# Weight buffers at four offsets modulo 128 bytes, and 13 warm-up products in place of 6

## What is computed

```python
def reference(x, mem, ..., c_2, ..., w_down_2):
    x = first_block(x, mem, g_mix, w_in, ...)     # retention + forgetting attention, w_out,
                                                  # cross attention to 256 memory rows, gated FFN (2816)
    return second_block(x, c_2, w_ada_2, ...)     # modulation from c, grouped attention + window pooling,
                                                  # w_out, FFN with a 3-tap convolution (2 x 2816)
```

## Time and profile before

| | us |
|---|---|
| median of three runs | 1438.58 |
| the three runs | 1436.09, 1438.58, 1439.15 |
| the profiled execution, first to last instruction | 1441.5 |
| TensorE busy in it | 1390.7 |
| VectorE busy | 818.5 |
| ScalarE busy | 616.9 |
| GpSimd busy | 604.1 |

### The profile page before, as it was taken

How to read it: one execution, slowest core, us unless ns; L and a number is a source line. 1 busy time by engine, 2 the same in 40 slices (tenths; PEclk the granted TensorE clock), 3 DMA queues, 4 the chain that set the end, 5 groups by cost and what they waited for, 6 DMA issues and landing times.

```text
span 1441.5 us, 17910 instructions
## 1 busy us (share of the span) xinstructions
PE 1390.7 (96%) x6628; PEld 1110.5 (77%) x6628; DVE 818.5 (57%) x1235; ACT 616.9 (43%) x857; POOL 604.1 (42%) x448
## 2 busy tenths in 40 slices
PE   8999999999999999999999889988999999999999
PEld 6877955788876888888888667864678888888887
DVE  5334948365342487777789994579355554553000
ACT  5455228543353343343431113578435555453111
POOL 3344320474521444544453444331344455556453
PEclk9999999999989999999999998999999999999999
DMA  7222221142210243333445553210121322222322
GB/s 262 86 87 95 80 67 51 59 149 106 88 68 1 90 170 149 131 140 140 156 162 188 205 190 107 83 59 30 59 88 59 116 87 87 100 104 88 117 88 88
DMA packets 28769, 154.20 MB, mean 107 GB/s; under 512 B 2992, under 2 KB 4144, under 8 KB 14512
## 3 DMA queue, kind: packets, MB, share of 16 engines
q1 hardware_dynamic: 28720, 153.52, 29.8%
HBM read 151.41 MB, written 2.10 MB: 106 GB/s over the span
## 4 chain that ended last, share of the span: by engine, by line
issue 41%; PE 30%; POOL 24%; DVE 4%; DMA 1%; POOLq 0%; ACT 0%; SPq 0%
POOL wlo L362 24%; PE lin L1326 10%; PE lin L1328 9%; PE lin L1327 9%; DVE small L992 1%; DVE expd L1003 1%; DMA raw<-w_slabs 1%; PE lin L1529 0%; PE att L1382 0%; DVE xl L872 0%; DVE win L1216 0%; DVE small L996 0%; POOLq L371 0%; DVE wlo L880 0%; PE att L1391 0%
## 5 line engine op out<-in xcount | busy, mean ns | idle before, releaser
L362 POOL TENSOR_TENSOR wlo<-raw,whi 128x512 fp32r<-128x512 f32 x444 | 603.9, 1391 | 821.4 <-ACT whi L389 546.4
L1326 PE MATMUL lin<-xh,whi 128*128 128x512 f32 x1072 | 423.6, 395 | 7.3 <-POOL wlo L362 3.6
L1328 PE MATMUL lin<-xh,wlo 128*128 128x512 f32 x1072 | 418.6, 390 | 0.0
L1327 PE MATMUL lin<-xl,whi 128*128 128x512 f32 x1072 | 418.3, 390 | 0.0
L1326 PEld LDWEIGHTS lin<-xh,whi 128*128 128x128 f32 x1072 | 202.0, 188 | 55.5 <-issue 9.5
L389 ACT ACTIVATE whi<-raw 128x2048 fp32r<-128x2048 f32 x66 | 126.5, 1917 | 254.7 <-PE lin L1328 202.1
L1328 PEld LDWEIGHTS lin<-xh,wlo 128*128 128x128 f32 x1072 | 201.9, 188 | 42.9
L1327 PEld LDWEIGHTS lin<-xl,whi 128*128 128x128 f32 x1072 | 202.1, 189 | 41.2 <-issue 0.5
L1326 PE MATMUL lin<-fh,whi 128*128 128x512 f32 x352 | 142.2, 404 | 6.3 <-POOL wlo L362 6.2
L1327 PE MATMUL lin<-fl,whi 128*128 128x512 f32 x352 | 141.3, 401 | 0.0
L1328 PE MATMUL lin<-fh,wlo 128*128 128x512 f32 x352 | 141.1, 401 | 0.0
(11 more groups left out here) (294 smaller groups left out, 1969.0 us busy)
## 6 DMA issues: line engine op xcount, KB each, us to landing
raw<-w_slabs SPq DMA_DIRECT2D x111, 1024.0 KB, 4.8
adar<-ada SPq DMA_DIRECT2D x48, 512.0 KB, 3.3
h<-x_t SPq DMA_DIRECT2D x4, 512.0 KB, 6.3
decay<-decay SPq DMA_DIRECT2D x4, 512.0 KB, 8.6
out_t<-h SPq DMA_DIRECT2D x3, 512.0 KB, 8.1
raw<-w_slabs SPq DMA_DIRECT2D x4, 256.0 KB, 7.8
rope<-rope SPq DMA_DIRECT2D x2, 512.0 KB, 7.3
memx<-mem_t SPq DMA_DIRECT2D x1, 1024.0 KB, 5.9
```

The source lines that it names most:

```text
L362: return nc.gpsimd.tensor_tensor(wlo[s][:, ks, :], raw[s][:, ks, :], f(whi[s][:, ks, :]), ALU.subtract)
L1326: nc.tensor.matmul(out, whi_, xhi_, start=first, stop=False)
L1327: nc.tensor.matmul(out, whi_, xlo_, start=False, stop=False)
L1328: return nc.tensor.matmul(out, wlo_, xhi_, start=False, stop=last)
```

## The change

The two `whi` are placed at 0 and 64 modulo 128 bytes and the two `wlo` at 32 and 96, by rounding the place up to 128 and adding the offset; what follows starts again at a multiple of 128. Everything from `par` on moves up by 384 bytes per partition, so that its place modulo 128 stays what it was. The loop of warm-up products runs 13 times in place of 6. No instruction is added otherwise, none changes its shape, and no wait changes.

```diff
-        whi = [sb(f"whi{i}", [P, KT, COLS], F32R) for i in range(2)]
-        wlo = [sb(f"wlo{i}", [P, KT, COLS], F32R) for i in range(2)]
+
+        def staggered(name, past):
+
+            base = -(-at[0] // 128) * 128 + past
+            at[0] = base + 4 * KT * COLS
+            return sb(name, [P, KT, COLS], F32R, offset=base)
+
+        whi = [staggered(f"whi{i}", past) for i, past in enumerate((0, 64))]
+        wlo = [staggered(f"wlo{i}", past) for i, past in enumerate((32, 96))]
+        at[0] = -(-at[0] // 128) * 128
         par = sb("par", [P, PARAMS["end"]])
...
             pe.wait_ge(par_in, 16)
-            for _ in range(6):
+            for _ in range(13):
                 nc.tensor.matmul(att[2][:, 0:COLS], par[:, 0:P], par[:, 0:COLS], start=True, stop=True)
```

## The result

The changed kernel takes 1449.03 us, the median of 4 runs (1445.14 to 1450.07); the kernel before, in runs beside it, 1437.76 (1436.09 to 1439.15, 4 runs). The ratio is 1.0075, with a 95% interval of 1.0059 to 1.0091: slower by 11.3 us, where 3.3 us faster was forecast. (One slip of the text ahead of the prediction: the weights come in 112 slabs, 111 transfers of 1 MB and a first slab in four quarters, and not in 114.)

A forecast was written before the change was run, and what follows sets the result against it. TensorE was taken as the bound, through its product count and step. Warm-up -3.0, `xh` products +4.9 and `fh`/`xah` products -5.2 sum to -3.3 us: median from 1438.58 to 1435.3 us, range 1418 to 1452.

The forecast's parts named there:

- What bounds the kernel: Whole kernel: TensorE, busy 1390.7 of 1441.5 us; number of products and their step, which seems to depend on operand places.
- Part 1: Start: 13 warm-up products fill TensorE's 3.13 us idle before the first slab, clock stays up; -3.0 us.
- the other bound: Start: with a later clock rise, added passes cost up to 5.9 us, slab 2.8 us late, about nothing gained.
- Part 2: Weight buffers at four places modulo 128: +4.9 us for products with `xh` moving, -5.2 us with `fh` and `xah`.
- (2 x 226.7 + 229) / 3 = 227.5: Even slabs with `xh` moving: step as mean over two `whi` loads and one `wlo` load, +0.8 ns.
- nearest row: Unmeasured step for `wlo` at 32 or 96: 229 ns, taken from `xh` moving against forget weights at 64.
- Part 2, `fh` and `xah`: Products with `fh` or `xah` moving: 231.9 ns in even slabs, 227.5 in odd; mean -3.6 ns x 1440, -5.2 us.
- The 384 bytes change no other place modulo 128: Buffers behind the weights: moving them up by 384 bytes keeps their places modulo 128; no size of its own.
- The third case: `xh` slabs: the good step needs all loads at one place and is lost; 1449.4 us, 1443 to 1457, chance 0.25.
- The second case: `wlo` loads at 32 and 96 stop meeting the stream, step near 213 ns; 1410 to 1429 us, chance 0.22.
- the fourth: All slabs: placement does nothing, the 6.6 ns belong to something else, only the warm-up gain remains; 1435.6 us, chance 0.15.
- The slabs with 256 columns, at nothing: Some 770 products with 256 columns: placement effect set at nothing, within 2 us.

The follow-up runs named there:

- places 32/96: Both weight buffers of even slabs at 32 modulo 128, of odd slabs at 96, 6 warm-up products, against the kernel before: 1456.04 us, ratio 1.013.

## Why the prediction was wrong

**What bounds the kernel: right.** The end moved with TensorE's steps; the other engines' busy time and the waits that the view shows say nothing of the 11 us. That the place of moving and stationary operand sets the step was right, and moving the region alone (226.7 against 233.3 for the same `fh`) shows it. A rule of the Trainium skill, SBUF — State Buffer, section Who interferes with whom, says that TensorE never waits on anyone. These runs show steps of 226.7 to 234.3 ns for one shape at full clock, according to where its own two operands lie, and by the rule the change of places alone would have cost nothing, where it cost 11.9 us; the measurement decides.

**Part 1: the step that failed is the size.** Its mechanism came as put down: the idle time went, the clock stayed, the forget products began at 21.74 against 21.9. But -3.0 was worked out from one execution, whose first slab ended 13.8 us after its first quarter was ready, the longest of nine starts with 6 products; the mean is 12.4. The late rise named as the other bound is common (after 7.9 us in four of the nine), and the added passes then overrun, by 1.6 us in one of three starts with 13; in the other two the slab starts 0.4 and 0.9 us after its quarter. Measured: -0.4. A smaller slip is the pass of 0.226 us: 3.62 us for 16 includes the drain of the last one, and the starts of two passes at full clock are 0.216 us apart, so 14 passes are 3.0 us and not 3.2.

**Part 2: the step that failed is "(2 x 226.7 + 229) / 3 = 227.5".** With `xh` moving, it gave +0.8 ns in even slabs and +2.3 in odd ones; measured were +6.6 (233.3) and +4.3 (231.0) in settled stretches, and +6.0 and +4.4 as means over all steps under 0.3 us. Three faults lie in it. One is the form: the step isn't a sum over loads, as the slab with `whi` 0 and `wlo` 128 shows (231.4 in place of 228.6). The next is the value of 229 for a `wlo` at 32 or 96, taken from the "nearest row". That row is the only favourable distance apart from 0: the six others tested give 232.4 to 234.3. The prediction itself said that it decides from 231 on. The last is the 229 for `whi1` in odd slabs: in the earlier trace rows the forget weights lie at 192 modulo 256, 64 below the stream, while `whi1` lies 64 above it, and on that side a step with all loads there is 233.3.

**Part 2, `fh` and `xah`: near in sum, wrong in each half.** Forecast 231.9 in even and 227.5 in odd slabs, measured 228.6 and 233.3; the mean over all products is 231.3, 2.0 ns less than before, and not 3.6, that is -2.9 us and not -5.2. "The 384 bytes change no other place modulo 128" was true and beside the point, since the period is 256: they moved the region from -64 to +64. That gave the even slabs 4.7 ns, where 1.4 were forecast. In the odd slabs `whi1` and the region are at one place indeed, and distance 0 for all loads is worth 226.7, but `wlo1`, 32 off, took all of it.

**The sum, with measured terms.** +5.2 ns x 3216 = +16.8; -2.0 x 1440 = -2.9; -0.4: +13.5 us, against 11.3 measured. Of the 2.2 us between, 1.8 lie where the prediction had no term: at the ten even slabs from 80 to 98, in the last large group with `xh`. In the kernel before, GpSimd ends the low part at 1135.52 + 3.45 = 1138.97 us, the slab's first product starts at 1139.10, 0.30 us after the product ahead of it, and the next one 0.33 us later:

```profile
1135.52 3.45 POOL L362 TENSOR_TENSOR wlo<-raw,whi 128x512 fp32r<-128x512 f32 x2
...
1138.80 0.39 PE L1328 MATMUL lin<-xh,wlo 128*128 128x512 f32 x1
...
1139.10 0.49 PE L1326 MATMUL lin<-xh,whi 128*128 128x512 f32 x1
...
1139.43 0.39 PE L1327 MATMUL lin<-xl,whi 128*128 128x512 f32 x1
```

It is the same at all ten: 0.13 us from GpSimd's end to the product, then the two long steps. These are waits for GpSimd that the view of waits doesn't count, since the record of the product ahead outlasts them. In the changed kernel the low part is made 0.25 us before the slab's first product instead of 0.13, and the two steps are 0.23 us each. TensorE's slower count hides what it waited for, 0.18 us at each of the ten slabs. Of the two large waits that the view does show, 3.6 us shorter together, only a part reaches the end: those for `expd` fell by 1.7 us between slabs 72 and 74, and with the change of places alone that stretch lasts 62.4 us in place of 62.8.

**The rivals.** The third case, the rhythm, comes nearest to what happened: 1449.4 forecast, 1449.03 measured, and its sign, a restless step through whole slabs, stands in the timeline (after, even slab: 230, 240 and 230 ns in the four rows below). Its own terms were less exact than the result: 231.7 for every product with `xh` is in fact 233.2 and 231.4, and its 3.0 us of warm-up were 0.4; that the sum fits to 0.4 us is luck. As put down, the good step needs all loads at one place, and that alone is not enough (233.3 with places 32/96): it must be the stream's.

```profile
1240.22 0.39 PE L1334 MATMUL lin<-xh,whi 128*128 128x512 f32 x1
1240.45 0.40 PE L1335 MATMUL lin<-xl,whi 128*128 128x512 f32 x1
1240.69 0.40 PE L1336 MATMUL lin<-xh,wlo 128*128 128x512 f32 x1
1240.92 0.39 PE L1334 MATMUL lin<-xh,whi 128*128 128x512 f32 x1
```

The argument that spoke for it was the earlier trace rows: after a disturbance the steps are 231.7 and settle later, though all loads have their good place. A table of single loads can't give that, and it should have weighed more than the smooth mean over a table. The second case falls (no distance runs below 226.7), and the fourth falls.

**The slabs with 256 columns, at nothing: right in sum.** From the first to the last product of each, the twelve slabs take 90.7 us before and 90.7 after: the four with `xh` stationary are 0.6 us quicker together, the eight of the memory 0.6 slower. What stays open is the circuit behind the rhythm: the runs show the period, the sign and that loads don't add up, but not what in the chip makes it so.

## What to carry to other kernels

Where back-to-back products bound a kernel, read the settled step between starts, stage by stage, and if two stages with one shape differ, move one operand alone and look again: here one line that puts the second streamed region at the weights' place modulo 256 gives 0.5%. Place the streamed operands and all stationary operands of a 512-column fp32r chain at one residue modulo 256 bytes; spreading them apart is what costs. Don't average a price per load when steps show memory of their neighbours, and don't size a change at the start from a single execution whose clock can rise at different moments.

## What the runs showed of the hardware

- The step of a 128x512 fp32r product depends on the places in SBUF of its stream and of the next loads, modulo 256 bytes: 226.7 ns at one place for all, 228.6 to 234.3 at any other arrangement tried, by the distance and not by the places themselves; 256 apart is like 0, 128 apart is not (232.4).
- The distance has a sign: 229 with the stream 64 ahead, 233.3 with it 64 behind.
- One load in three at another place can cost as much as all three (233.3, `wlo` at +96 or -32).
- With 256 columns it goes the other way: 120 ns at one place, 113 at -64 in three slabs and 118 in a fourth.
- The granted clock rose for the first time at moments from 6.1 to 8.8 us in profiles of the same beginning. After an idle time of 1.3 to 1.9 us ahead of the first slab it stayed up (four starts), after 2.1 to 2.9 us it was low for 3.4 us (three), and after 3.1 to 3.7 us for 6.8 us (three).
